# Delta-rule scan: TensorE's large products placed one by one between the small level products

## The reference

```python
m = where(strict, einsum('bhncd,bhnsd->bhncs', k_beta, k) * decay, 0)
t_inv = triangular_solve(eye + m, eye, lower=True, unit_diagonal=True)
def step(state, inp):
    v_new = u_i - einsum('bhcd,bhde->bhce', w_i, state)
    o = einsum(q_i * exp(g_i), state) + einsum('bhcs,bhse->bhce', a_i, v_new)
    state = state * exp(g_last) + einsum('bhcd,bhce->bhde', k_dec, v_new)
```

## Time and profile before

| | us |
|---|---|
| median of three runs | 3298.97 |
| the profiled execution, whole | 3303.14 |
| its span, first to last instruction | 3301.2 |
| from the first keys' product of the scan (tile 0) to that of tile 15 | 406.03 |
| of that, the first step (tile 0) | 39.21 |
| the remaining fourteen steps | 366.82 |
| a quiet step in the middle | 25.2 |

### The profile page before, as it was taken

How to read it: one execution, slowest core, us unless ns; L and a number is a source line. 1 busy time by engine, 2 the same in 40 slices (tenths; PEclk the granted TensorE clock), 3 DMA queues, 4 the chain that set the end, 5 groups by cost and what they waited for, 6 DMA issues and landing times. The chain is left out here.

```text
span 3301.2 us, 55530 instructions
## 1 busy us (share of the span) xinstructions
PE 3007.6 (91%) x20982; PEld 2493.2 (76%) x20982; DVE 1842.0 (56%) x3267; ACT 1233.4 (37%) x2500; POOL 556.1 (17%) x475
## 2 busy tenths in 40 slices
PE   7997998796999979969859999999999989979799
PEld 6886997685888975648648888878888857758687
DVE  5655442174677756655385677575676445543433
ACT  5222333152344328821152323343323367720132
POOL 0000000152234320033112233242332200000000
PEclk9998999895899899979969999999999989989899
DMA  4222764253344434046453212353223261154543
GB/s 135 86 67 103 249 231 144 83 157 106 122 152 140 137 113 133 27 153 205 159 194 110 95 64 96 128 169 106 83 71 103 92 203 53 33 194 175 191 146 121
DMA packets 289615, 423.30 MB, mean 128 GB/s; under 512 B 41568, under 2 KB 178784, under 8 KB 284256
## 3 DMA queue, kind: packets, MB, share of 16 engines
q1 hardware_dynamic: 238784, 379.68, 34.4%
q10 hardware_dynamic: 50592, 40.38, 3.8%
HBM read 270.56 MB, written 149.42 MB: 127 GB/s over the span
## 5 line engine op out<-in xcount | busy, mean ns | idle before, releaser
L113 PE MATMUL pj_pp<-h_hi,pj_whi 128*128 128x512 f32 x1152 | 450.6, 391 | 5.7 <-POOL h_lo L2873 5.5
L114 PE MATMUL pj_pp<-h_lo,pj_whi 128*128 128x512 f32 x1152 | 449.3, 390 | 0.0
L115 PE MATMUL pj_pp<-h_hi,pj_wlo 128*128 128x512 f32 x1152 | 449.2, 390 | 0.0
L113 PEld LDWEIGHTS pj_pp<-h_hi,pj_whi 128*128 128x128 f32 x1152 | 216.9, 188 | 52.6 <-issue 7.8
L115 PEld LDWEIGHTS pj_pp<-h_hi,pj_wlo 128*128 128x128 f32 x1152 | 216.9, 188 | 45.3
L114 PEld LDWEIGHTS pj_pp<-h_lo,pj_whi 128*128 128x128 f32 x1152 | 217.0, 188 | 44.5
L2700 ACT CAST pj_whi<-w_raw 128x512 fp32r<-128x512 f32 x192 | 119.2, 622 | 326.1 <-PE pj_pp L115 315.1
L2764 DVE TENSOR_TENSOR pj_wlo<-w_raw,pj_whi 128x512 fp32r<-128x512 f32 x192 | 160.8, 838 | 13.3 <-ACT pj_whi L2700 10.3
L113 PE MATMUL np_pp<-h_hi,np_whi 128*128 128x512 f32 x384 | 150.3, 391 | 0.0
L115 PE MATMUL np_pp<-h_hi,np_wlo 128*128 128x512 f32 x384 | 149.7, 390 | 0.0
L114 PE MATMUL np_pp<-h_lo,np_whi 128*128 128x512 f32 x384 | 149.7, 390 | 0.0
(11 more groups left out here) (345 smaller groups left out, 7425.5 us busy)
## 6 DMA issues: line engine op xcount, KB each, us to landing
w_raw<-in_w_second SPq DMA_DIRECT2D x192, 256.0 KB, 2.8
ds_pk<-scratch_pack SPq DMA_DIRECT2D x32, 1280.0 KB, 8.1
scratch_pack<-rp_out SPq DMA_DIRECT2D x32, 512.0 KB, 2.7
scratch_sig_fm<-pj_ob SPq DMA_DIRECT2D x64, 256.0 KB, 2.1
mb_sg<-scratch_sig_fm SPq DMA_DIRECT2D x16, 1024.0 KB, 7.3
rp_fm<-scratch_qkv_fm SPq DMA_DIRECT2D x96, 128.0 KB, 2.8
scratch_qkv_fm<-np_acc SPq DMA_DIRECT2D x11, 1024.0 KB, 4.8
np_acc<-in_x SPq DMA_DIRECT2D x16, 512.0 KB, 4.3
```

Of the source, the lines that this page charges most:

```text
L113: nc.tensor.matmul(out, ah, bh, start=(first and i == 0), stop=False)
L114: nc.tensor.matmul(out, ah, bl, start=False, stop=False)
L115: mm = nc.tensor.matmul(out, al, bh, start=False, stop=(last and i == n - 1))
```

## The change

- TensorE's list is written anew. Each large group of one direction stands alone between two small groups; only the `query_new` of direction 1 is cut further, into twice two heads, around `last_x`. `row` moves to the front of the step.
- The outputs go to PSUM bank 1 and `last_y`'s transposed half to bank 3, the two having been the other way round.
- The copies of the near halves into `uf` move from VectorE to ScalarE (`copy_near`); VectorE's and ScalarE's lists are reordered to go with TensorE's.
- The pack of tile i+2 is loaded as soon as the keys' product of tile i is done and the values are gated; the gates are loaded by themselves, with a semaphore of their own.
- TensorE's first `row` waits for the identity alone, no longer for all constants, and VectorE's presets stand ahead of its wait for the constants.

```diff
             def step(j, b, more):
                 i = 2 * j + b
+                if more > 1:
+                    for d in D:
+                        sp.wait_ge(v_gated[d], i + 1 + START)
+                        sp.wait_ge(ks_done[d], i + 1 + START)
+                        load_pack(i + 2, b, d)
...
-                    if more > 1:
-                        sp.wait_ge(state_done[d], i + 1 + START)
-                        load_pack(i + 2, b, d)
...
-            sp.dma_start(ident[:], consts[:, C_ID * P:(C_ID + 1) * P]).then_inc(const_in, 16)
+            sp.dma_start(ident[:], consts[:, C_ID * P:(C_ID + 1) * P]).then_inc(ident_in, 16)
...
+            def copy_near(i, b, d):
+                act.wait_ge(u_copied[d], i * NL + NL + START)
+                act.wait_ge(vnew_done[d], i + START)
+                for g in B:
+                    ins = nc.scalar.copy(uf[d][at_half[g], :, at_half[g]], u[d][b][at_half[g]])
+                ins.then_inc(uf_copied[d], 1)
...
-            def query_new(i, b, d):
+            def query_new(i, b, d, at):
                 pe.wait_ge(a_ready[d], i + 1 + START)
-                for h in range(4):
-                    mm = nc.tensor.matmul(ps[d][:, 3, cols[h]], a_t[d][b][:, h, :], vnew[d][:, h, :], start=False,
+                pe.wait_ge(vnew_copied[d], i + 1 + START)
+                for h in at:
+                    mm = nc.tensor.matmul(ps[d][:, 1, cols[h]], a_t[d][b][:, h, :], vnew[d][:, h, :], start=False,
...
+                ys(0)
+                if more > 1:
+                    for d in D:
+                        pe.wait_ge(t_copied[d], i + 1 + START)
+                        row(i + 2, d)
+                us(0)
+                state_keys(i, j, b, 0)
+                ys(1)
+                state_keys(i, j, b, 1)
+                us(1)
...
+                key_values(i, b, 0)
+                ys(4)
+                key_values(i, b, 1)
+                us(4)
+                query_new(i, b, 0, range(4))
                 if more:
                     last_y(i + 1, 1 - b)
-                query_state(i, b, 1, more)
-                key_values(i, b, 1)
+                query_new(i, b, 1, range(2))
                 if more:
                     last_x(i + 1)
-                query_new(i, b, 0)
-                query_new(i, b, 1)
-
-            pe.wait_ge(const_in, 16 * N_CONST_DMA + START)
+                query_new(i, b, 1, range(2, 4))
+
+            pe.wait_ge(ident_in, 16 + START)
```

More of the change, by code:

```diff
@@ L1142, in step, with turns, fills @@
                 i = 2 * j + b
-                for n in range(NL):
+                def turns(n):
                     if more:
                         for d in D:
-                            if n > 0:
-                                turn(i + 1, 1 - b, n, d)
+                            turn(i + 1, 1 - b, n, d)
+                def fills(n):
+                    if more:
+                        for d in D:
                             fill(i + 1, n, d)
[L1149 to L1160, removed]
-                        last_level(i + 1, 1 - b, d)
-                if more > 1:
-                    lower(i + 2, b, 1)
+                fills(0)
+                turns(1)
+                state_term(i, b, 0)
+                fills(1)
+                state_term(i, b, 1)
+                turns(2)
+                if more > 1:
+                    lower_decay(i + 2, b, 0)
+                fills(2)
+                if more > 1:
+                    lower_beta(i + 2, b, 0)
+                    first_level(i + 2, b, 0)
+                turns(3)
+                if more > 1:
+                    first_turn(i + 2, b, 0)
+                fills(3)
+                if more > 1:
+                    lower_decay(i + 2, b, 1)
+                    lower_beta(i + 2, b, 1)
+                turns(4)
+                next_state(i, b, 0)
+                fills(4)
+                if more > 1:
                     first_level(i + 2, b, 1)
@@ L1166, in step @@
                 next_state(i, b, 1)
+                if more:
+                    for d in D:
+                        last_level(i + 1, d)
+            for d in D:
+                nc.vector.memset(state[d][:], 0.0).then_inc(preset, 1)
+                nc.vector.memset(uf[d][:], 0.0).then_inc(preset, 1)
             dve.wait_ge(const_in, 16 * N_CONST_DMA + START)
@@ L1189, in _ @@
                     for d in D:
-                        lower(1, 1, d)
+                        lower_decay(1, 1, d)
+                        lower_beta(1, 1, d)
             for d in D:
-                last_level(0, 0, d)
+                last_level(0, d)
+            for d in D:
                 first_level(1, 1, d)
@@ L1240, in copy_o, with copies @@
                 act.wait_ge(stored[d], 16 * i + START)
-                nc.scalar.copy(ob[d][:], ps[d][:, 3, :]).then_inc(o_copied[d], 1)
+                nc.scalar.copy(ob[d][:], ps[d][:, 1, :]).then_inc(o_copied[d], 1)
             def step(j, b, more):
                 i = 2 * j + b
-                for n in range(NL):
-                    if more > 1:
-                        if n == 2:
-                            row_exponent(i + 2, b, 0)
-                        if n == 3:
-                            differences(i + 2, 1, 0)
-                        if n == 4:
-                            row_exponent(i + 2, b, 1)
+                def copies(n):
                     if more:
@@ L1406, in step, with us @@
                             level_y(i + 1, 1 - b, n, d)
-                    if n == 0:
-                        for d in D:
-                            state_keys(i, j, b, d)
-                    if more > 1 and n == 1:
-                        for d in D:
-                            pe.wait_ge(o_copied[d], i + START)
-                            row(i + 2, d)
-                    if n in (2, 3):
-                        new_values(i, n - 2)
-                    if n == 4:
-                        query_state(i, b, 0, more)
-                        key_values(i, b, 0)
+                def us(n):
                     if more:
```

110 lines of the change are left out of this document (63 added, 47 removed).

## The result

| | before | changed |
|---|---|---|
| median of five runs each, us | 3297.50 (3286.14 to 3299.95) | 3271.07 (3266.95 to 3278.23) |
| the profiled execution | 3303.14 | 3278.23 |
| first keys' product of the scan begins at | 805.79 | 800.87 |
| from there to that of tile 15 | 406.03 | 378.17 |
| from there to the span's end | 2089.4 | 2097.4 |

The ratio is 0.9931, with a 95% interval of 0.9911 to 0.9952: faster by some 26 us (0.7%), where 3534 us was forecast. Of the 24.9 us between the two profiled executions the loop gives 27.9 and the start 4.9; what follows the loop takes 8.0 more. That last part holds the stages which the change leaves alone.

The account below looks back on a forecast made before the run. TensorE was taken to set the pace, its clock deciding in the first step. Loop +234.1, last step +2.7 and start -3 gave +233.8 on 3303.1, 3536.9; the median, 4.2 lower, was put at 3534, range 3400 to 3562.

Parts of the forecast that it names:

- The step that failed: TensorE's new order: no adjacent pair left, so 1.2 GHz until the last step; +234.1 us over the loop.
- the first rival: Scan's clock rises early, at the end of the first or second step: -33, 3270 us; chance 0.10.
- A step at full clock: Scan step at 2.4 GHz: busy 23.35 us plus 0.1 for each of six more breaks, 23.95 us.
- Fourteen steps: Scan steps behind the first, at full clock: 14 x 23.95 - 1.02 = 334.3 against 366.82, -32.5 us.
- The forecast's 640.1: Fifteen scan steps at half clock, the last without `row`: 15 x 42.80 - 1.90 = 640.1 us.
- The first step: Scan's first step, if the clock rises early: 42 instead of 39.2 us, entered as +2.3.
- The half-clock step: One scan step at 1.2 GHz, summed from group lengths: 42.80 us, ends 42.1 to 43.2.
- The start: TensorE's first group no longer waits for the masks' load: at most 4.2 us, taken as -3.
- The last step: Scan's end: begins at 1.2 GHz, with two to four large groups before the rise; +2.7 us.
- zero for the loads: Earlier pack load removes GpSimd's wait, said not to end on TensorE; TensorE covers everything, so 0 us.
- Zero for the moved copies: `copy_near` on ScalarE adds 1.5 us there, but TensorE's 42.8 us step covers it: 0 us.
- VectorE as the bound (3283): Full clock, but VectorE's lower products beside GpSimd make TensorE 0.9 us late per step: 3283 us; chance 0.03.

Follow-up runs that it names:

- experiment 1: Two kernels without the computation: TensorE alone runs the scan's product shapes and the old and changed steps, each stretch begun at 1.2 GHz; no time against a kernel.
- near_dve: The changed kernel with the copies into `uf` back on VectorE: 3302.83 us, loop 407.53.
- experiment 6: The changed kernel with TensorE's first row and VectorE's presets waiting for all constants again: 3278.97 us, loop 377.46.
- near_act: The kernel before with only the copies into `uf` moved, to the front of ScalarE's step: 3270.18 us in one run.
- pairs: The changed kernel with its large groups in adjacent pairs again, the tail left as it is: 3249.56 us, ratio 0.9872.
- the old kernel, warmed: The kernel before with products of the identity by itself added in TensorE's idle time at the scan's start: 3298.11 us, ratio 1.0026.
- late_pack: The changed kernel with the pack and second gates load back at the step's end, behind the stored output: 3305.31 us in one run.

## Why the prediction was wrong

**The step that failed** is the first of the change's parts: "So of what the trace shows before every rise, nothing remains ... I therefore take it that the clock stays at 1.2 GHz from the scan's first product to the last step". It rested on five rises, all with an adjacent pair of large groups. The pair is one way up; `last_y` and `last_x` are another: each alone lifted the clock within 3 to 4 us (experiment 1), and the changed order has both of them packed with `query_new` at each step's end. Two of the five rises had L1356 in front of them. (The third came in the small group right behind the pair, at 920.4, and not inside L1381 as I wrote; that changes nothing.) I had noted this as a rival and gave it 0.10. Its mechanism is what happened, but the near match of its 3270 with the median of 3271.07 is partly luck: it was worked out for the profiled execution, which took 3278.23 because 8.0 us came behind the loop. Like with like, its -33 stands against the -32.8 of loop and start, and there too the terms differ and make up for each other.

The half of the argument that I drew from the earlier trace rows holds: a busy TensorE isn't enough, and small groups with single large ones between them do not lift the clock, in 92.5 us. What I left out is that they keep it once it is up (86 us in experiment 1, 338 us in the changed kernel). With that, one rise serves for the whole loop. My argument looked only for what lifts the clock and had no term for what keeps it.

The Trainium skill (TensorE: Matmul & The Clock Gate, "The HAM clock gate") has sustained activity release the throttle; with activity read as busy time, experiment 1 contradicts it, at 1.2 GHz through 92.5 busy us, as the earlier trace rows did. Its time, that of the first rival, came out all the same, because the tail's joins did what the busy alternation didn't.

**The terms of that rival**, now those of the result:
- A step at full clock: 23.95 forecast, 24.43 measured. It missed 0.23 of wait for VectorE's L1128 and 0.25 in the switches between large and small.
- Fourteen steps: 334.3 against 337.84. No fall of the clock, as it said. The longer steps would give some 7 us more; 3 of them are made up by an omission. I took one `row` away, but the last two steps lack one each, and the last lacks two small groups too (23.43 and 21.21 us). The forecast's 640.1 has the same omission, 5.5 us at half clock.
- The first step: 42 against 40.33, since the clock rose 3.8 us before its end. (42 less 39.2 is +2.8, where I wrote +2.3; the sum stays -33.) The half-clock step itself was forecast at 42.80 and takes 43.4 us of busy TensorE (`near_dve`), outside my ends of 42.1 to 43.2.
- The start: -3, measured -4.9 between the profiles and -6 in experiment 6.
- The last step: +2.7 went with the failed step; its stretch has the same 14.18 us as before.

**"GpSimd's wait for the pack ... does not end on TensorE", and zero for the loads: wrong.** It ends on TensorE by way of `dec` and ScalarE's queue. I looked for who waits for GpSimd's result and not for who waits for the buffer that GpSimd frees. In the changed kernel the late pack costs the loop 30.4 us, more than the loop's whole gain of 27.9.

**Zero for the moved copies: wrong at full clock.** They are worth 0.83 us a step, and in the one run without them the rise came a step later. VectorE as the bound (3283) did not come about: the lower products take 0.68 to 1.07 us in the changed kernel, and TensorE is late by 0.23 a step, not 0.9. With the copies back on VectorE the wait has about that rival's size, 1.06: the lost copies, which I had set against the rival, are what keeps it away.

**Where the gain comes from**, then: not from dealing out the large products, which costs 0.75 us a step and some 15 us by a later rise. It comes with fewer stalls of TensorE and with the falls of the clock that no longer follow them; the early pack and the moved copies each remove such stalls. Step by step, the four steps with a fall took 115.9 us before and take 97.7 now, the other ten 251.0 and 240.1: 18.2 and 10.8, the 29.0 us by which the fourteen steps are shorter (366.82 - 337.84). A quiet step is 1.0 us shorter, so that about 14 of the 18.2 belong to the falls themselves, as the forecast had counted. How the gain divides between load, copies and the rewritten lists is not shown: taking the early load or the moved copies away cost the whole of it each time, in one run each, and the copies alone, in the old lists, brought as much in one run.

**Open.** Why the first tail of `near_dve` passed at 1.2 GHz, when those of the changed kernel and all ten of experiment 1 did not; 0.14 us of idle time ahead of its L1395 is the only difference I found. Why the old order lifts the clock within 7.1 us in eight of eight of experiment 1 and in the first step of `near_act`, and not in that of the kernel before; so the 15 us of `pairs`' early rise rest on one profile. Why the old kernel, warmed, gained nothing over its ten runs. How much of `near_act`'s 30 us is its early rise. The swap of the two PSUM banks was not tried alone, nor was the early load in the old lists.

## What to carry to other kernels

When an engine waits long for a load, look at what it frees as well as at what it makes: putting the load back late cost the changed kernel 30.4 us here, through a buffer and two queues. What keeps a clock up may not be what lifts it, so from a trace that holds only rises, read also which mixtures the clock survived. Try each part of a rewritten order alone: the one that gives this change its name was a loss inside a gain, and putting the pairs back brought some 20 us more (0.9872 against 0.9931).

## What the runs showed of the hardware

- What kept TensorE's clock up did not lift it: the same alternation of small and large groups stayed at 1.2 GHz for 92.5 us from cold, and at 2.4 GHz for 86 us behind eight large groups.
- Three kinds of work, each alone, lifted it from cold within 3 to 4 us: large groups, the 64 x 64 joins of `last_y` with 64 columns, and `last_x`'s products. The old order, a small group with a pair behind it, did in 4.1 to 7.1 us, but not at the same place of the kernel before. The level products, 64 x 64 with 32 columns, did not in 68 us.
- It fell behind short stalls: all 14 falls in the loops of the kernel before, warmed and not, of `near_act` and of `late_pack` come within 2 us behind a stall of 0.60 to 1.71 us in front of a `level_y` group. Not every such stall does it: one of 1.25 us at 1040.95 in the kernel before, one of 1.52 at 1089.46 in `late_pack` and twelve of 1.06 to 1.12 at the tails of `near_dve` passed at full clock. The longest time down was the 24 us in `late_pack`.
- Changing between small and large groups costs TensorE 0.18 us for each pair that is split in two (4.28 against 4.10 us), at full clock.
